# One layer of a hybrid decoder on one core: each SSD group's end in another order, and the q and k squares summed in two fp32r parts

## Chip, core and metric

One core of a Trainium2 chip runs the whole layer. The metric is the device time of one execution in microseconds (us). The kernel before took 1418.91 us, median of 3 runs (1418.65 to 1421.53).

## What is computed

512 prompt tokens and 8 sequences of 8 sample tokens (T = 576 columns in all) go through one layer. Cut to what matters here:

```python
h = rmsnorm(x, norm1_w); q, k, v, z, xbc, dt, ga, gb = split(h @ w_in)
q = rmsnorm(q per head of 64) * q_norm_w; k likewise       # first stage
attn = stick_breaking_attention(q, k, v)
xs, B, C = split(silu(causal_conv(xbc)))                   # width 4
y = ssd_chunked(xs, dt, A, B, C) + d_skip * xs             # 4 groups of 8 heads
y = rmsnorm(y * silu(z), per group of 512 channels) * ssd_norm_w
merged = sigmoid(ga) * (attn @ w_pa) + sigmoid(gb) * (y @ w_pb)
x = x + merged @ w_out; x = x + swiglu(rmsnorm(x)) @ w_down
```

## The kernel before

Channels lie on partitions and tokens along the free axis, in two halves of 288. A weight product is exact to nearly fp32: the weights are loaded as fp32, ScalarE copies them to fp32r (`w_hi`, L455, make_hi), VectorE subtracts to get the rest (`w_lo`, L461, make_lo), and TensorE adds hi*hi, hi*lo and lo*hi (L487, L488, L491). One tile of 128 output channels takes 8 slices of 6 matmuls of 288 columns. Output tiles alternate between two PSUM tiles (G), so tile t waits (`tile_free`) until tile t-2 was read. Small results rotate through four spare banks. Weight chunks have two buffers. make_hi(c+1) needs the products of chunk c-1 done, and TensorE begins a chunk when make_lo for it is done (`split`). Every engine runs its own list, strictly in the written order.

**First stage (L1173, L1805, L2400).** 13 tiles, of which 10 are q and k. For each of the 10, VectorE copies the tile to `pre` (L2407), ScalarE squares it (L1813), TensorE multiplies the squares with a matrix of ones of the head pair, in fp32 (L1152, norm_sums, two matmuls), and ScalarE makes the root (L1767, L1773). Per iteration ScalarE does: make_hi, root, square, split q. VectorE: make_lo, copy, norm, split q.

**Ahead of group 0.** The six conv inputs of group 0 (B, C, four x tiles; `group_inputs(0)`) are made as tiles. For each, GpSimd copies the saved 3-token heads (L955, conv_head) and, once ScalarE has put the tile into `conv_src` (L2031 to L2033), takes tails (L963, L965, conv_tail). VectorE convolves in 4 operations (L2570, L2572), ScalarE applies silu (L2003). GpSimd also stores the decay sums (L1015, L1016) and reads rows of them back (L995, L998, L1006), before the heads of the second conv input.

**A group (L1560).** by_token turns xs; the chunk steps c = 0 to 3 and the sample step mix small SSD products with slices of weight tiles that `ssd_plan` names. Its last two entries are the group's end. For groups 0 to 2, plan[4] is the conv inputs x2 and x3 of the next group. Plan[5] is two z tiles in group 0, and the double tile pb3 and one z tile in groups 1 and 2 (pb is y @ w_pb, 4+4 slices into two tiles). In the last group plan[4] is empty and plan[5] is pb2, pb3. The end runs so: TensorE: x2, outputs, x3, turn of the state (L1596), first tile of plan[5], the sums of y squared (L1607, 8 fp32 matmuls with `ones`), 4 slices of the next tile, by_token (L1431), in which the other 4 slices are mixed. VectorE: convolution of x2 and x3, gating y*z (L2770), make_lo and reads, y scaled (L2780), xdt (L2624), y_lo (L2787), make_lo, y begun (L2634), cb and decay products (L2638, L2671). ScalarE: squares (L2154), make_hi between the second and third, root (L2162, L2166), y_hi (L2171). At L1509 TensorE needs the decay product.

**Last group and what follows.** VectorE adds the stored gates (L2613, L2614; add_gated) for k = 2, 3 before y is scaled. GpSimd waits for all four of these (L1071), issues four loads (L1073) and the store of the state (L1075), then four stores of conv rows (L1080, L1081), waits until they have landed, loads x again (L1089, 2 MB, and L1090) and then the gates of k = 4, 5 (L1094), which VectorE needs at L2812. Only after that step comes make_lo of the first chunk of w_out and with it the output stage (L1632).

## Time and profile before

| | us |
|---|---|
| median of 3 runs | 1418.91 |
| the profiled execution, its own time | 1418.91 |
| its span | 1417.4 |
| TensorE busy | 1351.2 (95%) |
| VectorE busy | 963.0 (68%) |
| ScalarE busy | 707.4 (50%) |
| GpSimd busy | 263.5 (19%) |

The span is 1.5 us shorter than the execution's time. Busy times are unions of instruction spans. TensorE's matmuls overlap in the records (a record of 0.29 us follows the one before it by 0.13 us), so a stretch is read from start to start. A bracket at the end of a timeline row gives the idle time ahead of it and what ended it.

### The profile page before, as it was taken

Reading aid. Unit: us, or ns where it says so; the run is one execution under the profiler, and the core shown is the slowest. Engines: PE = TensorE matmul, PEld = TensorE weight load, DVE = VectorE, ACT = ScalarE, POOL = GpSimd, SP = SyncE. Lnnn points to the kernel's source line nnn. Section 1 sums busy time; section 2 is a strip of 40 time slices with the busy share of each in tenths; the row PEclk is TensorE's granted clock in tenths of the full one; section 3 lists DMA queues with packets and bytes.
Section 4 is the critical chain, followed back from the end, with each engine's and each line's share of the span. In section 5 each row is a group of like instructions: output and inputs, shape, how many; then the busy total and the mean of one; then the engine's idle time right before and its main releaser. Section 6 shows DMA issues by size and latency. Waiting matters only on the chain. (4 is left out here: it accounts for less than half of the span.)

```text
span 1417.4 us, 26926 instructions
## 1 busy us (share of the span) xinstructions
PE 1351.2 (95%) x10301; PEld 1257.5 (89%) x10301; DVE 963.0 (68%) x1569; ACT 707.4 (50%) x1271; POOL 263.5 (19%) x467
## 2 busy tenths in 40 slices
PE   5999999999999899999999999999999999999996
PEld 4998777899999898888888887899999999999996
DVE  4455546788853476787787776877899999983221
ACT  4576445777632354574464464535644444452221
POOL 4002233000021423333333324211100000000000
PEclk9999999999999999999999999999999999999998
DMA  4226665122255333334334425362333333323331
GB/s 122 75 77 193 180 209 163 56 71 71 71 159 166 75 86 109 95 96 116 107 95 124 109 68 176 111 204 75 90 90 90 104 105 90 90 71 98 97 95 36
DMA packets 200897, 152.86 MB, mean 108 GB/s; under 512 B 15529, under 2 KB 187585, under 8 KB 200720
## 3 DMA queue, kind: packets, MB, share of 16 engines
q1 hardware_dynamic: 175394, 97.93, 24.5%
q0 software_dynamic: 24992, 52.85, 12.7%
q8 instruction: 83, 1.36, 0.4%
q10 hardware_dynamic: 384, 0.37, 0.1%
q14 instruction: 44, 0.35, 0.1%
HBM read 127.80 MB, written 23.29 MB: 107 GB/s over the span
## 5 line engine op out<-in xcount | busy, mean ns | idle before, releaser
L487 PE MATMUL tile_banks<-x_hi,w_hi 128*128 128x288 f32 (+1 forms) x1232 | 368.1, 314 | 11.5 <-DVE w_lo L461 10.1
L488 PE MATMUL tile_banks<-x_lo,w_hi 128*128 128x288 f32 (+1 forms) x1104 | 309.7, 296 | 0.0
L491 PE MATMUL tile_banks<-x_hi,w_lo 128*128 128x288 f32 (+1 forms) x1232 | 262.4, 294 | 0.0
L487 PEld LDWEIGHTS tile_banks<-x_hi,w_hi 128*128 128x128 f32 (+1 forms) x1232 | 231.7, 188 | 25.2 <-DVE w_lo L461 12.4
L461 DVE TENSOR_TENSOR w_lo<-w_raw,w_hi 128x1024 fp32r<-128x1024 f32 (+2 forms) x125 | 150.5, 1204 | 113.0 <-ACT w_hi L455 112.4
L488 PEld LDWEIGHTS tile_banks<-x_lo,w_hi 128*128 128x128 f32 (+1 forms) x1104 | 207.7, 188 | 5.5 <-issue 3.6
L491 PEld LDWEIGHTS tile_banks<-x_hi,w_lo 128*128 128x128 f32 (+1 forms) x1232 | 197.5, 187 | 0.4
L455 ACT ACTIVATE w_hi<-w_raw 128x1024 fp32r<-128x1024 f32 (+2 forms) x125 | 129.5, 1036 | 99.2 <-PE tile_banks L491 94.0
L488 PE MATMUL tile_banks<-f_lo,w_hi 128*128 128x288 f32 x352 | 98.6, 294 | 0.0
L1102 POOL DMA_DIRECT2D out_y_prompt<-y_tok x8 | 6.2, 778 | 386.1 <-ACT y_tok L2315 373.3
L2203 ACT ACTIVATE w_hi<-sum_raw 128x512 fp32r<-128x512 f32 x71 | 44.9, 634 | 60.3 <-PE tile_banks L1674 24.6
L488 PEld LDWEIGHTS tile_banks<-f_lo,w_hi 128*128 128x128 f32 x352 | 66.1, 188 | 0.0
L2572 DVE SCALAR_TENSOR_TENSOR conv_acc<-conv_src,conv_par,conv_acc 128x600 f32<-128x600 f32 x72 | 62.1, 862 | 2.5
L886 POOL DMA_DIRECT2D v_page<-in_cache_v x64 | 34.4, 537 | 154.4 <-issue 154.4
L487 PE MATMUL tile_banks<-y_hi,w_hi 128*128 128x288 f32 x192 | 56.1, 308 | 0.3 <-DVE w_lo L461 0.3
L487 PE MATMUL tile_banks<-t_blocks,w_hi 128*128 128x288 f32 x192 | 54.7, 300 | 1.6 <-DVE f_lo L2931 1.5
L488 PE MATMUL tile_banks<-y_lo,w_hi 128*128 128x288 f32 x192 | 53.8, 295 | 0.0
L2836 DVE TENSOR_TENSOR w_lo<-sum_raw,w_hi 128x512 fp32r<-128x512 f32 x71 | 49.9, 703 | 5.5 <-ACT w_hi L2203 5.5
L2031 ACT ACTIVATE conv_src<-tile_banks 128x288 f32<-128x288 f32 x24 | 9.9, 411 | 87.2 <-PE tile_banks L491 87.2
L2437 DVE TENSOR_TENSOR_SCAN after_w<-rest,zero_col 128x128 f32<-128x128 f32 (+2 forms) x64 | 52.3, 817 | 0.3
L1064 POOL DMA_DIRECT2D out_ssm_sample<-old x32 | 25.5, 797 | 118.1 <-DVE old L2717 108.0
L2439 DVE TENSOR_TENSOR beta<-beta,after_w 128x512 f32<-128x512 f32 (+2 forms) x80 | 42.6, 532 | 2.8
(490 smaller groups left out, 3678.1 us busy)
## 6 DMA issues: line engine op xcount, KB each, us to landing
w_raw<-in_w_in SPq DMA_DIRECT2D x68, 512.0 KB, 4.0
k_page<-in_cache_k SPq DMA_DIRECT2D x64, 128.0 KB, 2.6
v_page<-in_cache_v POOLq DMA_DIRECT2D x64, 128.0 KB, 3.0
old<-in_state_ssm POOLq DMA_DIRECT2D x32, 256.0 KB, 3.5
out_ssm_sample<-old POOLq DMA_DIRECT2D x32, 256.0 KB, 2.9
w_raw<-in_w_pb SPq DMA_DIRECT2D x16, 512.0 KB, 3.5
w_raw<-in_w_down SPq DMA_DIRECT2D x16, 512.0 KB, 4.0
gates_dram<-gate_out POOLq DMA_DIRECT2D x22, 288.0 KB, 2.8
```

The source lines that it names most:

```text
L455: nc.scalar.activation(w_hi[:, c % 2, 0:tiles, 0:width], w_raw[:, c % 2, 0:tiles, 0:width], ACT.Copy).then_inc(hi_made, 1)
L461: nc.vector.tensor_tensor(w_lo[:, c % 2, 0:tiles, 0:width], w_raw[:, c % 2, 0:tiles, 0:width], f32(w_hi[:, c % 2, 0:tiles, 0:width]), ALU. ...
L487: nc.tensor.matmul(out, wh, xh[:, HALVES[h]], start=start and k == 0, stop=False, skip_group_check=onto)
L488: nc.tensor.matmul(out, wh, xl[:, HALVES[h]], start=False, stop=False, skip_group_check=onto)
L491: mm = nc.tensor.matmul(out, wl, xh[:, HALVES[h]], start=False, stop=stop and k == last, skip_group_check=onto)
L886: eng.dma_start(v_page[:, n % V_SLOTS, :], cache_v[0, bass.ds(page_of(eng, x, k), 1)].rearrange("o p h d -> p (o h d)")).then_inc(sem(f"v_ ...
L1064: eng.dma_start(states_of(ssm_sample, g, b), old[:, b % 2]).then_inc(sem(f"state_stored{b % 2}"), 16)
L2203: eng.activation(form_slot(f)[0], form_raw(f), ACT.Copy).then_inc(sem("form_hi_made"), 1)
L2437: link(eng.tensor_tensor_scan(out=after_w[:, slot, edge - width:edge][:, ::-1], data0=rest[:, slot, cols][:, ::-1], data1=zero_col[:, 0:1] ...
L2439: return eng.tensor_tensor(beta[:, x["u"] % 4, cols], beta[:, x["u"] % 4, cols], after_w[:, slot, edge - width + 1:edge + 1], ALU.mult)
L2572: ins = eng.scalar_tensor_tensor(out=dst, in0=src[:, w:w + m], scalar=conv_par[:, w * CT + ct:w * CT + ct + 1], in1=dst, op0=ALU.mult, op1 ...
L2836: eng.tensor_tensor(low, form_raw(f), f32(high), ALU.subtract).then_inc(sem("form_split"), 1)
```

## The change

Groups' ends: x3's convolution moves behind the gating and the squares; ScalarE writes the four squares into four places, VectorE adds them (3 additions), and TensorE sums once per half (2 fp32 matmuls, waiting for `y_summed`). They stand after 6 slices of the first tile of plan[5], and 5 slices of the next tile go ahead of by_token. make_lo of the next chunk moves ahead of y_lo, and y begun behind the first decay product. In the last group TensorE does 2 slices of pb3 ahead of the sums, and add_gated((2, 3)) moves to the end. First stage: the squares are made twice (fp32r and fp32), VectorE subtracts, and TensorE uses 4 fp32r matmuls. Ahead of group 0 GpSimd's list is interleaved. The cut diff (by_token's slices are in its second argument list; `y_squares` names four existing buffers; take_pb is the old read of a pb tile, one half at a time; begin_y is the old L2633 to L2635):

```diff
@@ -1010,19 +1015,27 @@
+early_keys = group_inputs(0)
+for key in early_keys[0:2]:
+    conv_head(key)
 eng.wait_ge(sem("sums_split"), 4)
...
-conv_io(group_inputs(0)[0])
+conv_tail(early_keys[0])
 eng.wait_ge(sem("sums_out"), 16 * 6)
-for st in range(2):
-    sums_in(st)
-eng.wait_ge(sem("picks_made"), 1)
+sums_in(0)
+conv_tail(early_keys[1])
+conv_head(early_keys[2])
+sums_in(1)
+conv_tail(early_keys[2])
+conv_head(early_keys[3])
+eng.wait_ge(sem("sums_hi_made"), 3)
 for g in range(2):
     picks_in(g)
-for key in group_inputs(0)[1:]:
-    conv_io(key)
+    conv_tail(early_keys[3 + g])
+    conv_head(early_keys[4 + g])
+conv_tail(early_keys[5])
@@ -1145,11 +1158,12 @@
 def norm_sums(n):
 
-    pe.wait_ge(sem("squared"), n + 1)
+    pe.wait_ge(sem("squares_split"), n + 1)
...
-        pe.matmul(spare(key)[:, 0:HALF], pair_ones[:, :], sq[:, n % 2, HALVES[h]]).then_inc(bank_full[use[key][0]], 1)
+        pe.matmul(spare(key)[:, 0:HALF], pair_ones_r[:, :], sq_hi[:, HALVES[h]], start=True, stop=False)
+        pe.matmul(spare(key)[:, 0:HALF], pair_ones_r[:, :], sq_lo[:, HALVES[h]], start=False, stop=True).then_inc(bank_full[use[key][0]], 1)
@@ -1556,9 +1570,9 @@
 around = before_groups[-1]
-gemm(around, range(0, 4))
+gemm(around, range(0, 6))
 for g in range(NG):
-    by_token(g, around)
+    by_token(g, around, {3: range(5, 6), 4: range(6, 8)} if g else {3: range(6, 7), 4: range(7, 8)})
@@ -1595,25 +1609,24 @@
+    last = g == NG - 1
     for key in before:
-        gemm(key, range(3, KD) if g == NG - 1 else range(KD))
-
-    for j in range(PG):
...
-            mm = pe.matmul(spare(key)[:, 0:HALF], ones[:, :], conv_acc[:, j % 2, HALVES[h]], start=j == 0, stop=j == PG - 1, skip_group_check=True)
...
-    last = g == NG - 1
-    for key in later if last else later[:-1]:
-        gemm(key)
-    around = None if last else later[-1]
-    gemm(around, range(0, 4))
+        gemm(key, range(3, KD) if last else range(0, 6))
+    if last:
+        gemm(later[0], range(0, 2))
+
+    pe.wait_ge(sem("y_summed"), (PG - 1) * (g + 1))
+    for h in range(2):
+        key = ("y_ss", g, h)
+        wait_read(pe, key)
+        pe.matmul(spare(key)[:, 0:HALF], ones[:, :], y_squares[0][:, HALVES[h]]).then_inc(bank_full[use[key][0]], 1)
+    if last:
+        gemm(later[0], range(2, KD))
+        around = None
+    else:
+        gemm(before[0], range(6, KD))
+        around = later[0]
+        gemm(around, range(0, 5))
@@ -1802,15 +1815,17 @@
+eng.activation(pair_ones_r[:, :], pair_ones[:, :], ACT.Copy).then_inc(sem("squared"), 1)
...
         wait_freed(eng, c)
-        if c >= 2:
-            wait_full(eng, ("ss", c - 2, 1))
-        eng.activation(sq[:, c % 2, :], pre[:, c % 2, :], ACT.Square).then_inc(sem("squared"), 1)
+        if c >= 1:
+            wait_full(eng, ("ss", c - 1, 1))
+        eng.activation(sq_hi[:, :], pre[:, c % 2, :], ACT.Square).then_inc(sem("squared"), 1)
+        eng.activation(sq[:, :], pre[:, c % 2, :], ACT.Square).then_inc(sem("squared"), 1)
@@ -2137,24 +2152,28 @@
-    before, later = plan[NC]
-    for key in before + later:
+    before, late = plan[NC]
+    for key in before:
         slot(key)
+    for key in late:
+        next_hi(key)
     before, later = plan[5]
     flush()
-    eng.wait_ge(sem("conv_done"), 6 * min(g + 2, NG))
-    key = ("state_out", g)
-    wait_full(eng, key)
-    eng.wait_ge(sem("y_added"), NC * (g + 1))
-    eng.activation(state_out[:, :, :].rearrange("p j n -> p (j n)"), spare(key)[:, :], ACT.Copy).then_inc(bank_read[use[key][0]], 1)
+    eng.wait_ge(sem("conv_done"), 6 * (g + 2) - 1 if g < NG - 1 else 6 * NG)
     for j in range(PG):
+        if j == 2:
+            key = ("state_out", g)
+            wait_full(eng, key)
+            eng.wait_ge(sem("y_added"), NC * (g + 1))
+            eng.activation(state_out[:, :, :].rearrange("p j n -> p (j n)"), spare(key)[:, :], ACT.Copy).then_inc(bank_read[use[key][0]], 1)
         eng.wait_ge(sem("y_gated"), PG * g + j + 1)
-        if j >= 2:
-            eng.wait_ge(sem("y_summed"), 2 * g + j - 1)
-        eng.activation(conv_acc[:, j % 2, 0:T], y_t[:, j, :], ACT.Square).then_inc(sem("y_squared"), 1)
-        if j == 1:
-            for key in before:
-                slot(key)
+        if j == PG - 1:
+            eng.wait_ge(sem("y_summed"), (PG - 1) * g + 1)
+        eng.activation(y_squares[j], y_t[:, j, :], ACT.Square).then_inc(sem("y_squared"), 1)
+    for key in before:
+        next_hi(key)
+    for key in late:
+        empty(key)
@@ -2164,6 +2183,9 @@
     eng.activation(y_rinv, y_root, ACT.Exp, scale=-0.5).then_inc(sem("y_rooted"), 1)
+    flush()
+    for key in before:
+        empty(key)
@@ -2412,6 +2434,9 @@
         split_lo(c - 2)
+    if c < KD + 2:
+        eng.wait_ge(sem("squared"), 2 * (c + 1) + 1)
+        eng.tensor_tensor(sq_lo[:, :], sq[:, :], f32(sq_hi[:, :]), ALU.subtract).then_inc(sem("squares_split"), 1)
@@ -2739,6 +2772,8 @@
+        if c == 0:
+            begin_y(g)
         outputs(g, c)
         if c == 0:
             xend_lo(g)
@@ -2753,12 +2788,12 @@
-    before, later = plan[NC]
+    before, late = plan[NC]
     for key in before:
         slot(key)
     outputs(g, NC)
-    for key in later:
-        slot(key)
+    for key in late:
+        make_lo(chunk_of[key] + 1)
@@ -2768,11 +2803,21 @@
         eng.tensor_tensor(y_t[:, j, :], y_t[:, j, :], z_s[:, j, :], ALU.mult).then_inc(sem("y_gated"), 1)
+    for j in range(1, PG):
+        eng.wait_ge(sem("y_squared"), PG * g + j + 1)
+        if j > 1:
+            eng.wait_ge(sem("y_summed"), (PG - 1) * g + j - 1)
+        eng.tensor_tensor(y_squares[0], y_squares[0], y_squares[j], ALU.add).then_inc(sem("y_summed"), 1)
     before, later = plan[5]
     for key in before:
-        slot(key)
-    if g == NG - 1:
-        add_gated((2, 3))
+        if key[0] == "pb":
+            take_pb(key, 0)
+        make_lo(chunk_of[key] + 1)
+    for key in late:
+        empty(key)
+    for key in before:
+        if key[0] == "pb":
+            take_pb(key, 1)
@@ -2781,13 +2826,20 @@
     if g + 1 < NG:
         scale_tokens(g + 1)
+        for key in later:
+            make_lo(chunk_of[key] + 1)
...
     ins.then_inc(sem("y_split"), 1)
+    if g == NG - 1:
+        for key in later:
+            make_lo(chunk_of[key] + 1)
     for key in later:
-        slot(key)
+        empty(key)
+    if g == NG - 1:
+        add_gated((2, 3))
```

## Rows read from the trace of the kernel before

**Rows 1.** The page: span.

```profile
span 1417.4 us, 26926 instructions
```

**Rows 2.** Waits of TensorE, whole span: total us, times, longest.

```profile
PE tile_banks L487 <- DVE w_lo L461: 11.4, 8, 4.2
...
PE spare_bank L1473 <- DVE old L2717: 4.9, 13, 0.4
```

**Rows 3.** L1152's count, and L1607 in group 0's end (timeline: start, us, what).

```profile
L1152 PE MATMUL spare_bank<-sq,conv_out x40: 403/404/408, 41.3 to 107.8; 128*128 128x288 f32 x40
...
608.31 2.10 PE L1607 MATMUL spare_bank<-conv_acc,ones 128*128 128x288 f32 x8
...
612.42 0.51 PE L487 MATMUL tile_banks<-x_hi,w_hi 128*128 128x288 f32 x1
```

**Rows 4.** Timeline of one period of the first stage.

```profile
55.93 1.14 PE L1152 MATMUL spare_bank<-sq,conv_out 128*128 128x288 f32 x4
...
58.27 0.67 ACT L1813 ACTIVATE sq<-pre 128x576 f32<-128x576 f32 x1
...
60.70 1.06 ACT L455 ACTIVATE w_hi<-w_raw 128x1024 fp32r<-128x1024 f32 x1
...
61.80 1.22 DVE L461 TENSOR_TENSOR w_lo<-w_raw,w_hi 128x1024 fp32r<-128x1024 f32 x1 [0.91 <-ACT w_hi L455]
...
63.23 1.14 PE L1152 MATMUL spare_bank<-sq,conv_out 128*128 128x288 f32 x4
```

**Rows 5.** Timeline ahead of group 0; its last row is a window's granted clock.

```profile
473.24 0.59 DVE L2570 TENSOR_SCALAR conv_acc<-conv_src,conv_par 128x600 f32<-128x600 f32 x1 [3.80 <-POOL conv_src L955]
...
477.65 0.61 PE L487 MATMUL tile_banks<-x_hi,w_hi 128*128 128x288 f32 x1 [4.21 <-DVE w_lo L461]
...
483.06 0.59 DVE L2570 TENSOR_SCALAR conv_acc<-conv_src,conv_par 128x600 f32<-128x600 f32 x1 [5.47 <-POOL conv_src L955]
...
487.49 0.40 PE L487 MATMUL tile_banks<-x_hi,w_hi 128*128 128x288 f32 x1 [1.94 <-DVE w_lo L461]
...
512.06 1.09 PE L1436 MATMUL spare_bank<-ident,xs_t 128*128 128x128 f32 x8 [1.73 <-ACT xs_t L2004]
...
478.00:480.00 2.00, 2.00 (x10) 0.50 0.60 143
```

**Rows 6.** Timeline of group 1's end and group 2's beginning.

```profile
711.04 0.60 PE L1596 MATMUL spare_bank<-ident,state 128*128 128x128 f32 x4
...
711.24 0.41 ACT L2031 ACTIVATE conv_src<-tile_banks 128x288 f32<-128x288 f32 x1 [3.30 <-PE tile_banks L491]
...
712.05 0.60 DVE L2570 TENSOR_SCALAR conv_acc<-conv_src,conv_par 128x600 f32<-128x600 f32 x1 [1.51 <-ACT conv_src L2033]
...
715.22 2.75 DVE L2770 TENSOR_TENSOR y_t<-y_t,z_s 128x576 f32<-128x576 f32 x4
...
717.79 1.05 ACT L455 ACTIVATE w_hi<-w_raw 128x1024 fp32r<-128x1024 f32 x1
...
734.21 0.40 PE L487 MATMUL tile_banks<-x_hi,w_hi 128*128 128x288 f32 x1 [1.12 <-DVE w_lo L461]
...
739.21 0.99 PE L1509 MATMUL spare_bank<-decay,xdt 128*64 128x128 f32 x14 [0.66 <-DVE decay L2671]
```

**Rows 7.** Timeline of the last group's end up to the output stage.

```profile
911.61 1.22 DVE L461 TENSOR_TENSOR w_lo<-w_raw,w_hi 128x1024 fp32r<-128x1024 f32 x1 [0.37 <-ACT w_hi L455]
...
911.84 4.18 PE L1607 MATMUL spare_bank<-conv_acc,ones 128*128 128x288 f32 x16
...
917.38 0.55 POOL L1073 DMA_DIRECT2D xs_t<-gated_dram  x1 [13.02 <-DVE pb_sum L2614]
...
933.89 0.76 POOL L1089 DMA_DIRECT2D x_again<-in_x_prompt  x1 [5.42 <-DMA out_conv_sample<-xend]
...
946.23 0.76 DVE L2812 TENSOR_TENSOR conv_acc<-conv_acc,conv_src 128x576 f32<-128x576 f32 x1 [0.86 <-DMA conv_src<-gates_dram]
...
952.98 0.37 PE L487 MATMUL tile_banks<-m_hi,w_hi 128*128 128x288 f32 x1 [1.44 <-DVE conv_acc L2804]
```

More of the change, by code:

```diff
@@ L256, in build @@
         pre = sb("pre", [P, 2, T], F32, qkv)
-        sq = sb("sq", [P, 2, T], F32, qkv)
+        sq = sb("sq", [P, T], F32, qkv)
+        sq_hi = sb("sq_hi", [P, T], F32R, qkv)
         root = sb("root", [P, T], F32, qkv)
@@ L265, in build @@
         k_out = sb("k_out", [P, 5, NKV * HD], F32, qkv)
+        sq_lo = sb("sq_lo", [P, T], F32R, qkv)
+        pair_ones_r = sb("pair_ones_r", [P, P], F32R, qkv)
         qkv.close()
@@ L332, in build @@
         y_rinv = decay[:, 0:5, :].rearrange("p h l -> p (h l)")[:, 0:T]
+        y_squares = [y_rinv, y_root, conv_acc[:, 0, 0:T], y_root]
         ssd.close()
@@ L1427, in gemm, with by_token @@
                         mm.then_inc(tile_done, 1)
-            def by_token(g, key_after):
+            def by_token(g, key_after, parts):
                 pe.wait_ge(sem("conv_done"), 6 * (g + 1))
@@ L1437, in by_token @@
                     mm.then_inc(bank_full[use[key][0]], 1)
-                    if c in (1, 3, 4):
-                        gemm(key_after, {1: range(4, 6), 3: range(6, 7), 4: range(7, 8)}[c])
+                    if c in parts:
+                        gemm(key_after, parts[c])
                 b_t, c_t = bc_t[:, g % 2, 0, :], bc_t[:, g % 2, 1, :]
@@ L2404, in _ @@
                     if c >= 2:
-                        eng.wait_ge(sem("squared"), c - 1)
+                        eng.wait_ge(sem("squared"), 2 * (c - 1) + 1)
                         eng.wait_ge(sem("normed_made"), c - 1)
@@ L2587, in empty, with take_pb @@
                 elif key[0] == "pb":
-                    _, g, n0 = key
                     for n in range(2):
-                        wait_tile(eng, t + n)
-                        dst = halves(pb_sum[:, n0 + n, :])
-                        if g == 0:
-                            ins = eng.tensor_copy(dst, tile(t + n))
-                        else:
-                            wait_freed(eng, tile_of[("pb", g - 1, n0)] + n)
-                            ins = eng.tensor_tensor(dst, dst, tile(t + n), ALU.add)
-                        ins.then_inc(tile_free[(t + n) % 2], 1)
+                        take_pb(key, n)
+            def take_pb(key, n):
+                t = tile_of[key] + n
+                _, g, n0 = key
+                wait_tile(eng, t)
+                dst = halves(pb_sum[:, n0 + n, :])
+                if g == 0:
+                    ins = eng.tensor_copy(dst, tile(t))
+                else:
+                    wait_freed(eng, tile_of[("pb", g - 1, n0)] + n)
+                    ins = eng.tensor_tensor(dst, dst, tile(t), ALU.add)
+                ins.then_inc(tile_free[t % 2], 1)
             def make_xend(g, c):
@@ L2632, in by_token @@
                     eng.wait_ge(sem("y_split"), g)
-                for j in range(PG):
-                    eng.tensor_scalar(y_t[:, j, :], xs_t[:, j, :], par[:, PAR_D + g * PG + j:PAR_D + g * PG + j + 1], None, ALU.mult)\
-                       .then_inc(sem("y_begun"), 1)
                 key = ("cb", g)
@@ L2652, in by_token, with begin_y @@
                                   ALU.mult).then_inc(sem("xend_f_made"), 1)
+            def begin_y(g):
+                for j in range(PG):
+                    eng.tensor_scalar(y_t[:, j, :], xs_t[:, j, :], par[:, PAR_D + g * PG + j:PAR_D + g * PG + j + 1], None, ALU.mult)\
+                       .then_inc(sem("y_begun"), 1)
             def xend_lo(g):
```

11 lines of the change are left out of this document (1 added, 10 removed).

## The prediction

> **What bounds the kernel now.** I read the page, TensorE's waits, then TensorE's timeline beside VectorE's, ScalarE's and GpSimd's at the places that the diff touches. TensorE is busy 1351.2 us (the table above) of a span of 1417.4 [rows 1], so work taken from it counts in full, unless a wait takes its place. Its waits are small and named: the largest sum, 11.4 us in 8 waits, is for the second part of the weights, the longest 4.2 us [rows 2]. Prices: a period of the first stage is 7.30 us [rows 4]. An fp32 matmul of 288 columns leaves two records. Group 0's sums, 16 records, end where the next product starts, 612.42-608.31 = 4.11 us, 0.51 per matmul [rows 3]. So two of them take 1.03, and a tile of 48 fp32r matmuls 7.30-1.03 = 6.27: 0.13 each, 0.78 per slice.
>
> **First stage.** Ten norm sums (40 records [rows 3] are 20 matmuls) go from 2 x 0.51 to 4 x 0.13: TensorE could save 0.51 each. But ScalarE gets a second square (0.6 to 0.67 [rows 4]) ahead of the weights' first part, and VectorE a subtraction of 576 columns, 0.69 (as one of the four of L2770 [rows 6]), ahead of the second. Now make_hi starts 4.77 after the sums begin and make_lo ends at 63.02, 7.09 after [rows 4]. The root comes 0.24 earlier (the first half's sum is ready after 0.26, not 0.51), so make_hi ends near +6.2, and make_lo at +7.45. TensorE would want that chunk at 6.27+0.52+0.52 = 7.3. Cover lost by 0.15 us, shared by two periods: the period is 6.9, saving 0.4 ten times, **-4.0** with one more small copy. Bounds: 0 if queues stretch the period to today's, -5.1 if nothing waits.
>
> **Ahead of group 0.** VectorE's first convolution starts at 473.24 after 3.8 us for GpSimd's head copy, the second at 483.06 after 5.5 us [rows 5]. Both heads now come before GpSimd's stores of sums. VectorE was free at 473.24-3.80 = 469.4; I give ScalarE's copies of the tile 0.4 more. A convolution takes 715.22-712.05 = 3.2 [rows 6] and make_lo 1.2 [rows 4], so TensorE, which arrives at 473.4 (477.65-4.21), starts at 474.4 and the next tile at 474.4+6.3 = 480.7 instead of 487.49 [rows 5]. That is 6.8: waits of 3.3 and 1.9, and 1.5 of clock. After the wait of 4.21 the granted clock is 0.50, the level of 1.2 GHz, and the tile from 477.65 to 485.55 takes 7.9, not 6.3 [rows 5]. The wait of 1.73 for the last silu [rows 5] is covered by two more slices, 1.57. GpSimd's reads of rows then come later, but are wanted only after by_token, 30 us on. **-8.3**; at the least -5, if heads 3 and 4 come late.
>
> **Groups 0 to 2, the sums.** Six fp32 matmuls less: -3.1 each. ScalarE's squares (0.65) and VectorE's additions (0.69) must be there when TensorE arrives. In group 1 VectorE was free at 712.05-1.51 = 710.5 [rows 6], where gating now starts: it ends 2.8 later at 713.3. Squares 1 and 2 are made meanwhile, then the copy of the state (0.6) and square 3 (713.9); the first addition ends at 714.0, square 4 at 714.7, the last addition near 715.5; TensorE arrives after 6 slices, 711.45+4.7 = 716.2. Hidden.
>
> **The same, what is late next.** x3's tile, which ScalarE now reads at 711.24 [rows 6], is read only after the four squares and make_hi (1.05 [rows 6]): squares end at 714.7, make_hi 715.7, three copies 716.5. The second half of pb3 uses the same PSUM tile and is wanted after 4 slices, 711.45+3.15 = 714.6: a **new wait of 1.9** in groups 1 and 2. Group 0 has a z tile there, in the other PSUM tile: none. The waits of 1.12 at 734.21 [rows 6], one like it in each of the three groups, go, since make_lo moves ahead of y_lo and is done 1.5 before TensorE's need. The silu of x3 ends at about 723.0, by_token wants it at 724.7: hidden by 1.7. The decay product: now TensorE is there at 739.21-0.66 = 738.55, 4.3 after 734.21 [rows 6]. In the new order y_lo, cb (0.7), b (0.8), xend (0.7) and the product (1.2) bring VectorE to 4.6 after the next group's first product (make_lo is done 1.5 before it, y_lo takes 2.75): a wait of 0.3, not 0.66. y begun (1.8) now stands between that product and VectorE's next work, which I expect 0.55 later; TensorE's short waits for VectorE there (13 of at most 0.4 [rows 2]) grow by 0.5 in groups 1 and 2. Group 0's end: -3.1-1.1-0.2 (an old wait within its sums, part of the 4.11) -0.5+0.5 = **-4.4**. Group 1: -3.1-1.1+1.9-0.3+0.5 = **-2.1**. Group 2: -3.1-1.1+1.9-0.3 = **-2.6**; there eight slices stand ahead of the decay product and hide y begun, and a wait of 0.3 goes. Bounds for each: -4.5 with no new wait, 0 if the new waits are double.
>
> **Last group.** make_hi for pb3's weights stood after the second square, so VectorE's second part started at 911.61, in time [rows 7]. Now it follows the fourth square, which follows the first addition: make_hi ends at 913.6, VectorE adds to 913.3, reads one half of pb2 (0.7), make_lo to 915.2. TensorE is ready at 911.84 [rows 7]: a new wait of 3.4, and the sums after 2 slices at 916.9. They take 1.0, to 917.9, and pb3 ends 6 slices on, at 922.6, 0.5 later than now. The root takes 1.4 and y scaled 3.0, to 922.3, y_lo to 925.0, make_lo 926.2, two reads 927.6, and only then the four operations of add_gated, 3.0: 930.6. GpSimd waits for that; now it goes on at 917.38 [rows 7]. Behind it stand in its list 4 loads (0.55 each), a store (0.8), 4 small stores (0.53 each), their landing (5.4 [rows 7]), and then x again: 930.8+10.5 = 941.4 instead of 933.89. The gates behind x again are awaited by VectorE until 946.23 already now [rows 7]. They come 7.5 later, and with them make_lo for the output stage: TensorE, ready at 952.98-1.44 = 951.5 now [rows 7] and 1.6 later then (pb3's tile is read only at 926.9), starts it near 960.4. **+7.4.** The idle of 7 us brings the low clock again: after 4.21 us it cost 1.5 [rows 5]; I take **+1.4**. After 3.4 idle us it may fall too; the later idle hides that except for 1.
>
> By the Trainium skill's page "TensorE: Matmul & The Clock Gate" (Part 1), half the clock is the idle state and sustained activity releases it. By that rule both pauses of the last group start cold; by rows 5 the first is open. The sum with both is 1407.
>
> **Sum.** -4.0-8.3-4.4-2.1-2.6+8.8 = -12.6, against the profiled execution's own 1418.91 (span 1417.4 [rows 1] and 1.5 around it), which is also the median of the runs: 1406.3, I say **1406**.
>
> **Rivals.**
> *A, the forecast* (0.52; its own range 1401 to 1411).
> *B, GpSimd's late list costs nothing.* Add_gated moved, but if x again and the gates were quick (their 12.3 us from issue to use [rows 7] are for 2.8 MB), the output stage starts after TensorE's own delay of 1.6. Then -12.6-8.8+1.6: 1399. For: TensorE waits there only 1.44 now. Against: VectorE waited for just this load. 0.17.
> *C, VectorE's and ScalarE's longer lists bind more.* The first stage keeps its period (+4.0), and each of three group ends keeps its 1.1 us wait (+3.3): 1413.6. For: both lists have under 1.5 us of room in a period. Against: that room is read off the same rows. 0.19.
> *D, hardly a difference*, C with the gain ahead of group 0 halved by GpSimd (+4.2): 1418. 0.07.
> *E, slower: the low clock stays.* Place: the output stage, after the long idle. Price: 0.5 us for every us at 1.2 GHz. Ahead of group 0 the tile after the wait lost only 1.5 us, what 3 us at half the clock cost [rows 5]. If it stayed low for its eight tiles, 8 x 6.3 = 50 us more: 1456. It turns the forecast over once the low level lasts about 25 us longer. Nothing in the rows shows such a length. 0.03.
> *F, the change doesn't act where it says*: the sums wait for VectorE so long that what six matmuls saved is idle. Each of four ends loses its 3.1, -12.6+12.4: about 1419, in "same". The additions end 0.7 before need, so 0.02.
>
> **Chances.** 0.2% is 2.8 us, about what a measurement of this kernel tells from no change: within 1416.1 to 1421.7 is "same". Faster: A, B, C 0.88; same: D, F 0.09; slower: E 0.03. The range takes A's bounds and most of B and C: 1398.5 to 1413; D to F and the rest of C and B, under 0.2, lie outside.
>
> **What would show it.** Right: L1152 with 40 records of 0.29 us, period 6.9; L1607's successor with 16 records in all; no wait of 4.2 and no clock of 0.50 ahead of group 0; TensorE waiting about 1.9 us for ScalarE's conv_src copies in groups 1 and 2, within pb3; 3.4 us for make_lo ahead of pb3 in the last group; L1073's successor waiting for pb_sum until 13 us later relative to the sums; and at the output stage's first product some 7 us of idle time and a granted clock of 0.5. Wrong: no wait at the output stage (B), a period near 7.3 (C), group ends without the 1.9 (faster by 4). The largest term is GpSimd's list in the last group; if one figure breaks the forecast it is that one.

## The result, and the profile after

The changed kernel takes **1410.82 us** (median of 4 runs, 1410.58 to 1412.5) beside 1418.85 for the kernel before in the same runs: ratio 0.9944, 95% interval 0.9930 to 0.9957, a gain of 8.0 us. I had forecast 1406, a gain of 12.6, with a range of 1398.5 to 1413. The profiled execution of the changed kernel is its slowest run, 1412.5 us, with a span of 1411.0, so the spans differ by 6.4 us only.

TensorE's waits of the changed kernel (engine, line, what it waited for: us in all, times, longest):

```profile
PE tile_banks L492 <- DVE conv_acc L2854: 7.1, 1, 7.1
...
PE tile_banks L492 <- DVE w_lo L466: 6.1, 5, 3.4
...
PE tile_banks L492 <- ACT conv_src L2048: 3.0, 2, 1.6
...
PE spare_bank L1523 <- DVE decay L2704: 2.2, 2, 1.1
...
PE tile_banks L492 <- DVE conv_acc L2856: 1.8, 1, 1.8
```

The sum for the weights' second part is 6.1 in 5 waits, 11.4 in 8 before [rows 2]. Ahead of group 0 the waits of 4.21 and 1.94 have become one of 0.77; of the three of 1.1 at the groups' ends two are gone, and the third, behind group 2, is 0.59. New are 7.1 us for L2854, which I had not forecast, 3.4 for pb3's weights and 3.0 for ScalarE's copies, which I had.

To place the difference I read the starts of the same instructions in TensorE's two timelines (us from the span's start; a stretch ends at the instruction that its row names, and the last two columns are us gained in it):

| stretch, up to | start before | start after | gained | forecast |
|---|---|---|---|---|
| first product of the first stage | 20.68 | 20.14 | 0.5 | 0 |
| first stage, to the turning of v | 114.38 | 110.88 | 3.0 | 4.0 |
| attention, to the decay sums | 465.59 | 460.94 | 1.1 | 0 |
| ahead of group 0 and by_token, to its first sample step | 530.12 | 516.32 | 9.2 | 8.3 |
| group 0's end, to group 1's first sample step | 632.03 | 613.87 | 4.4 | 4.4 |
| group 1's end | 741.13 | 721.31 | 1.7 | 2.1 |
| group 2's end | 853.60 | 832.31 | 1.5 | 2.6 |
| last group's steps | 903.78 | 883.10 | -0.6 | 0 |
| last group's end, to the output stage's second turning of x again | 959.38 | 952.96 | -14.3 | -8.8 |

Behind that point the rest of the span is as long as before, within 0.02 us. Up to the last group's end 20.7 are gained for 21.4 forecast; 1.6 of them lie in the two stretches that the change does not touch and are no merit of it, and 0.6 are lost again in the last group's steps, in a wait for a load of old states (1.59 us, 0.96 before) that has nothing to do with the change either. The stretches that it does touch gain 19.8. In the last group's end 14.3 are lost, not 8.8. That figure is an upper end: the profiled execution is the slowest of the four, and three kernels of the experiments that have the same last group (e8_ends, e12_begin_early, e4_empty_early) take 66.43, 67.42 and 68.15 us for this stretch, where the kernel before takes 55.60 and the changed one 69.86. So the loss is 10.8 to 14.3 us.

The first stage: periods of 6.86 to 7.10 us, mean (104.02 - 41.57)/9 = 6.94, 6.9 forecast, 7.31 before by the same reading. make_lo ends 61.42 + 1.23 - 55.29 = 7.36 us after the sums begin (7.45 forecast):

```profile
41.57 0.29 PE L1165 MATMUL spare_bank<-sq_hi,pair_ones_r 128*128 128x288 f32 x1
...
55.29 0.29 PE L1165 MATMUL spare_bank<-sq_hi,pair_ones_r 128*128 128x288 f32 x1
...
61.42 1.23 DVE L466 TENSOR_TENSOR w_lo<-w_raw,w_hi 128x1024 fp32r<-128x1024 f32 x1
...
104.02 0.30 PE L1165 MATMUL spare_bank<-sq_hi,pair_ones_r 128*128 128x288 f32 x1
```

Ahead of group 0 neither convolution waits for GpSimd now: the first starts when ScalarE has filled its tile, the second straight behind VectorE's work before it. TensorE waits 0.77 us where it waited 4.21 [rows 5]:

```profile
465.22 0.59 DVE L2595 TENSOR_SCALAR conv_acc<-conv_src,conv_par 128x600 f32<-128x600 f32 x1 [0.42 <-ACT conv_src L2048]
...
469.64 0.40 PE L492 MATMUL tile_banks<-x_hi,w_hi 128*128 128x288 f32 x1 [0.77 <-DVE w_lo L466]
...
469.72 0.59 DVE L2595 TENSOR_SCALAR conv_acc<-conv_src,conv_par 128x600 f32<-128x600 f32 x1
...
499.84 0.33 PE L1450 MATMUL spare_bank<-ident,xs_t 128*128 128x128 f32 x1 [0.29 <-ACT xs_t L2019]
```

Group 1's end (timeline): the squares, the additions, make_hi behind the fourth square, and only then the copies of x3's tile, for which TensorE waits 1.57 in pb3's second half; later the decay product, 1.09. The last row is behind group 2's end, where a wait for make_lo is left:

```profile
696.20 0.69 ACT L2172 ACTIVATE old_t<-y_t 128x576 f32<-128x576 f32 x1 [0.32 <-DVE decay L2810]
...
696.80 1.04 ACT L460 ACTIVATE w_hi<-w_raw 128x1024 fp32r<-128x1024 f32 x1
...
697.74 0.39 ACT L2046 ACTIVATE conv_src<-tile_banks 128x288 f32<-128x288 f32 x1
...
697.08 0.76 DVE L2810 TENSOR_TENSOR decay<-decay,old_t 128x576 f32<-128x576 f32 x1
...
698.55 0.40 PE L492 MATMUL tile_banks<-y_hi,w_hi 128*128 128x288 f32 x1 [1.57 <-ACT conv_src L2048]
...
719.38 0.88 PE L1523 MATMUL spare_bank<-decay,xdt 128*64 128x128 f32 x12 [1.09 <-DVE decay L2704]
...
830.60 0.40 PE L492 MATMUL tile_banks<-y_hi,w_hi 128*128 128x288 f32 x1 [0.59 <-DVE w_lo L466]
```

The last group's end, by engines: TensorE's waits of 3.43, 1.33, 7.05 and 1.76; VectorE's wait for the store of the state; GpSimd's list.

```profile
894.78 0.61 PE L492 MATMUL tile_banks<-y_hi,w_hi 128*128 128x288 f32 x1 [3.43 <-DVE w_lo L466]
...
897.83 1.28 PE L1622 MATMUL spare_bank<-decay,ones 128*128 128x288 f32 x4
...
908.08 0.37 PE L492 MATMUL tile_banks<-y_last_hi,w_hi 128*128 128x288 f32 x1 [1.33 <-DVE pb_sum L2626]
...
921.71 0.58 PE L492 MATMUL tile_banks<-y_last_hi,w_hi 128*128 128x288 f32 x1 [7.05 <-DVE conv_acc L2854]
...
945.01 0.37 PE L492 MATMUL tile_banks<-m_hi,w_hi 128*128 128x288 f32 x1 [1.76 <-DVE conv_acc L2856]
...
919.67 1.23 DVE L466 TENSOR_TENSOR w_lo<-w_raw,w_hi 128x1024 fp32r<-128x1024 f32 x1 [8.15 <-DMA out_ssm_prompt<-e_t]
...
938.25 0.76 DVE L2864 TENSOR_TENSOR conv_acc<-conv_acc,conv_src 128x576 f32<-128x576 f32 x1 [1.18 <-DMA conv_src<-gates_dram]
...
911.82 2.16 POOL L1086 DMA_DIRECT2D xs_t<-gated_dram  x4 [28.14 <-DVE pb_sum L2644]
...
913.98 0.77 POOL L1088 DMA_DIRECT2D out_ssm_prompt<-e_t  x1
...
921.29 0.76 POOL L1102 DMA_DIRECT2D x_again<-in_x_prompt  x1 [4.50 <-DMA out_conv_sample<-xend]
...
923.86 1.12 POOL L1107 DMA_DIRECT2D conv_src<-gates_dram  x2 [1.28 <-DVE conv_acc L2861]
```

GpSimd goes on at 911.82, after 28.14 us for L2644, the last operation of add_gated. It stores the state (L1088) at 913.98; VectorE, which awaits the landing of all four stores of a state ahead of the weights' second part for the last product's next chunk, waits 8.15 us for it, until 919.67; TensorE waits 7.05 us for what VectorE then reads. x again (L1102) is issued at 921.29. The granted clock in windows of 2 us behind the waits of 3.43, 7.05 and 1.76 (columns: window, us, busy and instructions of PE, PEld, DVE, ACT, POOL, then the clock, the DMA share, GB/s):

```profile
894.78:896.78 2.00, 2.00 (x8) 2.00 (x9) 0.61 (x1) 0.00 (x0) 0.00 (x0) 0.50 0.39 112
896.78:898.78 2.00, 2.00 (x11) 1.84 (x9) 0.00 (x0) 0.12 (x1) 0.00 (x0) 0.67 0.44 151
921.71:923.71 2.00, 2.00 (x8) 2.00 (x9) 1.92 (x4) 0.78 (x2) 0.87 (x2) 0.50 0.74 237
923.71:925.71 2.00, 2.00 (x11) 2.00 (x10) 1.81 (x3) 1.52 (x2) 1.12 (x2) 0.57 0.81 277
945.00:947.00 2.00, 1.99 (x11) 2.00 (x12) 1.97 (x4) 0.00 (x0) 0.00 (x0) 0.73 0.71 214
947.00:949.00 2.00, 2.00 (x11) 2.00 (x10) 1.97 (x3) 1.20 (x2) 0.00 (x0) 0.50 0.21 57
949.00:951.00 2.00, 2.00 (x16) 2.00 (x16) 1.73 (x3) 1.72 (x4) 0.00 (x0) 0.92 0.00 0
```

A window at 0.50, the level of 1.2 GHz, loses 1.0 of its 2 us. By that measure the three stretches lose 1.7, 1.9 and 1.7 us, 5.2 in all. That nearly closes the account of the last end: idle 13.57 us for 1.85 before (0.41 ahead of the last product, and 1.44 [rows 7]) is +11.7, the sums 0.90 for 3.80 are -2.9, the clock +5.2: 14.0 of 14.3. (The sums take 0.76 us in group 1, at full clock, so 0.1 of the clock's share is counted twice.)

### The profile page after: what moved, and what is told of

It is laid out like the page before. It is cut to its first block and busy times, and to the rows that moved or that the text cites. A ratio compares the mean times of both kernels' runs of the same rounds, so it can differ in the third digit from the quotient of the medians.

```text
span 1411.0 us, 26872 instructions
## 1 busy us (share of the span) xinstructions
PE 1339.1 (95%) x10253; PEld 1250.8 (89%) x10253; DVE 981.3 (70%) x1591; ACT 711.5 (50%) x1282; POOL 262.8 (19%) x467
## 3 DMA queue, kind: packets, MB, share of 16 engines
q0 software_dynamic: 24992, 52.85, 12.6%
## 5 line engine op out<-in xcount | busy, mean ns | idle before, releaser
L492 PEld LDWEIGHTS tile_banks<-y_hi,w_hi 128*128 128x128 f32 x192 | 36.7, 191 | 9.9 <-DVE w_lo L466 4.5
```

The costliest lines, as they stand in the source:

```text
L492: nc.tensor.matmul(out, wh, xh[:, HALVES[h]], start=start and k == 0, stop=False, skip_group_check=onto)
```

## The experiments

Theory 1: the last group's loss hangs on GpSimd's list, which add_gated at the end holds up, and on the clock that falls behind the waits. Theory 2: it comes of the new order of squares, additions and sums. "The same stretch" below is the last row of the table, from the last group's last step to the second turning of x again. Each kernel ran beside the kernel before, whose median was 1418.3 (the first four kernels, e1 to e4), 1418.6 (e5, e7, e8, e9), 1419.3 (e6, e10, e11) and 1418.9 (e12); the changed kernel's 1410.82 stood beside 1418.85. Differences between kernels that ran at different times are uncertain by a microsecond or two: the intervals of the ratios say how much.

**add_gated back ahead of y scaled (e1_gated_back).**

```diff
@@ last group, VectorE @@
+                if g == NG - 1:
+                    add_gated((2, 3))
                 eng.wait_ge(sem("y_rooted"), g + 1)
...
-                if g == NG - 1:
-                    add_gated((2, 3))
```

> The changed kernel with one thing undone: the last group's add_gated((2, 3)) stands ahead of y scaled again, in the 5.06 us in which VectorE waits for the root. Theory 1 (GpSimd's list, held up by add_gated at the end, costs the last group its gain): GpSimd's four loads start near 898.5 instead of 911.8, VectorE's wait of 8.15 us for the store of the state and TensorE's of 7.05 behind it go, x again is issued near 916 instead of 921.3, the output stage starts 9.4 us earlier, and with the low clock after the wait gone 1.5 more: 1410.8 - 11 = 1400, between 1398.5 and 1402. Theory 2 (the wait only hides one for the loads of x again and of the gates, which are as late either way because they wait for the conv rows): TensorE's 7.05 us turn up at the output stage instead, 1408 to 1411.

Measured: **1400.28** (1399.16 to 1401.49), ratio 0.9867 (0.9853 to 0.9882). GpSimd and TensorE:

```profile
899.18 2.16 POOL L1086 DMA_DIRECT2D xs_t<-gated_dram  x4 [14.97 <-DVE pb_sum L2644]
...
901.33 0.76 POOL L1088 DMA_DIRECT2D out_ssm_prompt<-e_t  x1
...
915.42 0.76 POOL L1102 DMA_DIRECT2D x_again<-in_x_prompt  x1 [4.11 <-DMA out_conv_sample<-xend]
...
908.74 0.37 PE L492 MATMUL tile_banks<-y_last_hi,w_hi 128*128 128x288 f32 x1 [1.33 <-DVE pb_sum L2626]
...
895.35 0.40 PE L492 MATMUL tile_banks<-y_hi,w_hi 128*128 128x288 f32 x1 [3.43 <-DVE w_lo L466]
```

No wait for L2854 is left, the output stage starts at 935.40, and the clock there is 1.00. It is theory 1, with its number: one operation group's place costs 10.5 us by the medians, and 11.7 in the traces (the same stretch takes 58.20 us, 69.86 in the changed kernel). The wait of 3.43 stands as in the changed kernel, with a fall of the clock behind it: these are the new order's doing, and with them the stretch is still 2.6 us longer than before. To that extent theory 2 is right too.

**The store of the state ahead of the wait (e2_store_first).**

```diff
@@ GpSimd, last group @@
+                wait_after_read(eng, ("state_out", g))
+                eng.dma_start(ssm_prompt[...], state_out[:, :, :]).then_inc(sem("stored_prompt_state"), 16)
                     eng.wait_ge(sem("gated_added"), 4)
                     for k in range(4, KD):
                         eng.dma_start(gated_a(k), gated_dram[k]).then_inc(sem("gates_in0"), 16)
-                wait_after_read(eng, ("state_out", g))
-                eng.dma_start(ssm_prompt[...], ...)
```

> The changed kernel with GpSimd's store of the last state put ahead of its wait for add_gated((2, 3)); add_gated stays at the end. It parts the two things that stand behind add_gated: the store of the state, which VectorE awaits ahead of the last product, and the loads of x again and of the gates of k = 4, 5. If only the store counts (theory 1a): TensorE's 7.05 us and 1.5 of low clock go, 1402. If the loads are as late as my prediction had it (theory 1b): the 7.05 us go, but x again is still issued near 920.5, the gates are there near 933 and the output stage starts near 940 instead of 945, after a wait of 5 to 6 us in front of it: 1405 to 1407. Theory 2 as in the run before: no gain, 1410 to 1411.

Measured: **1409.22** (1406.77 to 1410.38), ratio 0.9929 (0.9913 to 0.9945). The store goes at 892.21 and the 7.05 are gone, but TensorE waits at the output stage, as I had forecast for the change itself:

```profile
892.21 0.75 POOL L1084 DMA_DIRECT2D out_ssm_prompt<-e_t  x1 [7.01 <-ACT e_t L2168]
...
922.56 0.76 POOL L1102 DMA_DIRECT2D x_again<-in_x_prompt  x1 [5.25 <-DMA out_conv_sample<-xend]
...
935.42 0.76 DVE L2864 TENSOR_TENSOR conv_acc<-conv_acc,conv_src 128x576 f32<-128x576 f32 x1 [6.23 <-DMA conv_src<-gates_dram]
...
942.17 0.58 PE L492 MATMUL tile_banks<-m_hi,w_hi 128*128 128x288 f32 x1 [6.81 <-DVE conv_acc L2856]
```

The clock is 0.50 behind that wait too. It is mechanism 1b. By the medians the kernel gains 1.6 us where I expected 4 to 6, and its interval overlaps the changed kernel's; by the traces the same stretch takes 65.53 us, 4.3 less, as expected, and this execution had merely come into the last group 1.5 later (884.61 for 883.10). From x again's issue to the first use of the gates 12.86 us pass here and 12.34 before [rows 7], but 16.96 in the changed kernel. The two consequences of the late list lie one behind the other; taking one away shows the other.

**add_gated late in the kernel before (e10_late_add).**

```diff
@@ the kernel before, last group, VectorE @@
-                if g == NG - 1:
-                    add_gated((2, 3))
                 eng.wait_ge(sem("y_rooted"), g + 1)
...
                 for key in later:
                     slot(key)
+                if g == NG - 1:
+                    add_gated((2, 3))
```

> The kernel before with one thing of the change: add_gated((2, 3)) moved to the end of the last group. Theory: VectorE would end it near 928.8, GpSimd's four loads (2.2 us) and the store of the state follow, the store lands near 936.5, and VectorE, which waits for it ahead of the second part of the next weights (926.85 now), holds TensorE up by some 6 us at the last product's second tile; with 1.5 us of low clock behind the wait and x again and the gates later the output stage is 7 to 10 us later: 1418.6 + 8.5 = 1427, between 1424 and 1430. Rival: by its position alone it costs little, and the changed kernel's loss in the last group comes of the new order of squares, additions and sums: below 1421.

Measured: **1426.53** (1424.85 to 1428.24), ratio 1.0049 (1.0031 to 1.0067): 7.3 us slower. Its rows are those of the changed kernel:

```profile
930.88 0.76 POOL L1075 DMA_DIRECT2D out_ssm_prompt<-e_t  x1
...
936.36 1.23 DVE L461 TENSOR_TENSOR w_lo<-w_raw,w_hi 128x1024 fp32r<-128x1024 f32 x1 [8.13 <-DMA out_ssm_prompt<-e_t]
...
938.40 0.58 PE L487 MATMUL tile_banks<-y_last_hi,w_hi 128*128 128x288 f32 x1 [6.93 <-DVE conv_acc L2802]
```

So the place alone makes this wait, without the new order, and theory 2 is out for this part.

**Each part of the change alone (e7_ahead, e8_ends, e6_first_stage).** The kernel before with a part of the diff each (the hunks are those shown ahead of the prediction):

```diff
@@ e7_ahead: GpSimd ahead of group 0, TensorE @@
+early_keys = group_inputs(0) ... conv_tail(early_keys[5])
+gemm(around, range(0, 6))
+by_token(g, around, {1: range(4, 6), 3: range(6, 7), 4: range(7, 8)} if g else {3: range(6, 7), 4: range(7, 8)})
@@ e6_first_stage: sq_hi, sq_lo, pair_ones_r @@
+eng.activation(sq_hi[:, :], pre[:, c % 2, :], ACT.Square).then_inc(sem("squared"), 1)
+eng.tensor_tensor(sq_lo[:, :], sq[:, :], f32(sq_hi[:, :]), ALU.subtract).then_inc(sem("squares_split"), 1)
@@ e8_ends: all the rest @@
+gemm(around, range(0, 4))
+by_token(g, around, {3: range(5, 6), 4: range(6, 8)} if g else {1: range(4, 6), 3: range(6, 7), 4: range(7, 8)})
```

> The kernel before with GpSimd's interleaved list ahead of group 0 and six slices instead of four there, and nothing else. My theory by the traces (the deltas between the two kernels there, 7.6 us up to by_token and 1.6 in it): 1418.3 - 9.1 = 1409.2, between 1407.5 and 1411. As forecast -8.3: 1410. Rival: a part of the 9.1 comes from the loads of cached pages, which shift stage 2 by 1 to 2 us from run to run: 1411 to 1413.

> The kernel before with the groups' ends rebuilt and nothing else (q and k squares as before, GpSimd's list ahead of group 0 as before). By the traces groups 0 to 2 gain 4.0, 1.7 and 1.9 and the last one loses 14.3, of which the part behind the end is x again's: 1418.3 + 4 to + 7, so 1422 to 1425, slower than before. By my prediction's terms (-4.4 - 2.1 - 2.6 + 8.8 = -0.3): 1418. Rival: the end's rebuilding is a gain on its own and the first stage's change a loss: below 1416.

> The kernel before with the q and k squares in two fp32r parts, and nothing else. By the traces the mean period of the first stage falls from 7.31 to 6.94 us, 3.3 over nine periods, and 0.5 to 0.8 come back in the first iterations: 1418.6 - 2.7 = 1415.9, between 1415 and 1417; the same figure is what is left when the run with only the list ahead of group 0 (-9.1) and the one with only the groups' ends (+3.9) are taken from the whole change (-7.8). My prediction had -4.0: 1414.6. Rival: the longer lists of ScalarE and VectorE give all of it back, 1418.6.

| kernel | median, us | ratio, 95% interval | against before |
|---|---|---|---|
| ahead of group 0 | 1409.51 | 0.9939 (0.9921 to 0.9956) | -9.1 |
| groups' ends | 1422.49 | 1.0026 (1.0015 to 1.0036) | +3.9 |
| first stage | 1414.80 | 0.9966 (0.9954 to 0.9977) | -4.5 |

The groups' ends, the largest part of the diff, are a **loss** on their own: one late list costs more than six matmuls a group bring. The first two rows are as expected. The third is larger than the changed kernel's trace gave it, and nearer to my prediction; its interval goes from -3.3 to -6.5, and its own trace gains 3.9 in the stretch of the first stage (89.79 us for 93.70). The three add up to -9.7 against -8.0 for the whole, which those intervals allow. Where between 3.0 and 4.5 it lies stays open.

**Copies of x3's tile ahead of the fourth square (e4_empty_early).**

```diff
@@ ScalarE @@
                     if j == PG - 1:
+                        for key in late:
+                            empty(key)
                         eng.wait_ge(sem("y_summed"), (PG - 1) * g + 1)
...
-                for key in late:
-                    empty(key)
```

> The changed kernel with ScalarE's three copies of x3's tile ahead of the fourth square, not behind make_hi (groups 0 to 2). Theory: TensorE's waits of 1.57 and 1.41 us for these copies in groups 1 and 2 go whole, since the fourth square and the last addition then end about when TensorE reaches the sums: 1410.8 - 3.0 = 1407.8. Rival: the sums wait instead, since VectorE's last addition comes 1 us later: the waits move there and the time stays within 1 us of 1410.8.

Measured: **1406.99** (1403.92 to 1409.81), ratio 0.9915 (0.9900 to 0.9929). Both waits for L2048 are gone, and no wait stands at the sums (L1622), so the rival is out. Two waits grow in their place: the decay product's behind group 1's end from 1.09 to 1.58, and the one for make_lo behind group 2's end from 0.59 to 1.28:

```profile
721.28 1.09 PE L1523 MATMUL spare_bank<-decay,xdt 128*64 128x128 f32 x16 [1.58 <-DVE decay L2704]
```

By the starts the two ends gain 2.7 us more than in the changed kernel; the median says 3.8, with an interval that allows both.

**pb3's weights early in the last group (e3_hi_early), and with them pb2's first tile (e9_read_early).**

```diff
@@ ScalarE, last group: behind square j == 1 (moved up from behind the last square) @@
+                        next_hi(pb3)
@@ VectorE, last group (both moved up from behind the additions) @@
+                take_pb(pb2, 0)         (only e9_read_early)
                 addition j == 1
+                make_lo(pb3's chunk)
                 additions j == 2, 3
```

> The changed kernel, in the last group alone: make_hi of pb3's weights after the second square and make_lo after the first addition, as the old order had it. Theory: of TensorE's wait of 3.43 us ahead of pb3 some 1.3 are left, too short for the clock to fall to 0.50 (which cost 1.6 more over the next two slices and the sums); everything behind it, GpSimd's list too, comes 3.5 us earlier: 1407.3, between 1406.3 and 1408.5. Rival: the wait moves to the sums, which then wait for the last addition, and the gain is below 1 us: 1410.

> The changed kernel, in the last group alone: as in the run with make_hi and make_lo earlier (where TensorE still waited 3.33 us ahead of pb3, now for VectorE's read of pb2's first tile, at 893.31), and that read moved ahead of the first addition too. Theory: pb3's first product waits for two things, its weights and the PSUM tile that pb2's first half leaves; with both early the wait is about 1.0 us, the low clock behind it goes, and all that follows is 3.5 to 4 us earlier than in the changed kernel: 1407, between 1406 and 1408. Rival: the wait then moves to the sums, behind the last addition, and less than 1.5 us is gained: 1409.5.

Measured: **1408.68** (1408.49 to 1412.05), ratio 0.9937 (0.9920 to 0.9953), for the first, **1406.29** (1403.20 to 1408.84), ratio 0.9913 (0.9894 to 0.9932), for the second. TensorE at pb3's first product in the one and in the other:

```profile
893.31 0.37 PE L492 MATMUL tile_banks<-y_hi,w_hi 128*128 128x288 f32 x1 [3.33 <-DVE pb_sum L2630]
```

```profile
890.86 0.40 PE L492 MATMUL tile_banks<-y_hi,w_hi 128*128 128x288 f32 x1 [1.70 <-DVE w_lo L466]
```

In the first the weights were ready, and the wait stayed at 3.33 us, now for VectorE's read of the PSUM tile, which stood behind the additions: neither my theory nor my rival had it. Two things were late at one place, and the profile named only the later. That kernel's 2.1 us are not clear of the changed kernel's interval. With both early the wait is 1.70 (1.0 expected), the clock stays at 1.00 behind it, and 4.5 us are gained, as the theory had it (1406 to 1408).

**Three orders together (e5_three), and a fourth (e11_four).** e5_three is e1_gated_back, e4_empty_early and e9_read_early in one kernel; e11_four adds:

```diff
@@ VectorE, last group, behind y_lo @@
+                take_pb(pb3, 0)
                 make_lo(chunk of the last product)
-                take_pb(pb3, 0)
                 take_pb(pb3, 1)
```

> The changed kernel with three orders mended: add_gated((2, 3)) ahead of y scaled (alone 1400.3), x3's tile copied ahead of the fourth square (alone 1407.0), and pb3's weights and pb2's first tile early in the last group. Theory: they stand at different places and add up: 1410.8 - 10.5 - 2.8 - 3.8 = 1393.7, between 1392 and 1396. Rival: in the last group the conv rows' stores set when x again is loaded (issued at 915.42 in the run with add_gated back), so the gain ahead of pb3 comes back as a wait at the output stage: 1397 to 1398.

> The kernel with three orders mended (1396.2) and a fourth: in the last group VectorE reads pb3's first tile ahead of make_lo for the last product, not both tiles behind it. In that kernel TensorE waits 0.86 us ahead of the conv rows' transposes and 1.33 ahead of the last product, for this read, and the granted clock is 0.50 in the 2 us behind them. Theory: the second wait falls to 0.6 and the clock stays at 1.00: 1396.2 - 0.7 - 1.5 = 1394.0, between 1393 and 1395.5. Rival: the clock falls all the same, or the last product waits for its weights instead: 1395.5 to 1396.5.

Measured: **1396.19** (1393.48 to 1397.32), ratio 0.9835 (0.9815 to 0.9854), and **1395.55** (1394.33 to 1399.99), ratio 0.9840 (0.9818 to 0.9862). Both beat the kernel before and the changed one; e11_four beats e5_three by less than the measurement's uncertainty. e5_three lies just outside the 1392 to 1396 that I expected. Its rival is out: the wait at the output stage is 0.49 us. The three gains of 10.5, 3.8 and 4.5 would make 18.8; together they are 14.6. In e5_three TensorE waits 0.86 us for ScalarE ahead of the conv rows and 1.33 ahead of the last product, and the clock behind the two is 0.50 (e1_gated_back, with the same 1.33 alone, has 1.00). The wait of 0.86, which none of the three has alone, and the low clock (1.6 us by the measure above) are 2.5 of the 4.2 us that are missing; the rest I could not place, and it is within what the medians leave uncertain.

```profile
900.38 1.10 PE L1635 MATMUL spare_bank<-ident,conv_out 128*27 128x128 f32 x8 [0.86 <-ACT xdt L2203]
...
902.81 0.58 PE L492 MATMUL tile_banks<-y_last_hi,w_hi 128*128 128x288 f32 x1 [1.33 <-DVE pb_sum L2630]
```

The fourth order moved that second wait by 0.09 only, from the tile to the weights, and the clock fell all the same: it is the rival that came true.

**y begun ahead of the cb product again (e12_begin_early).**

```diff
@@ VectorE, by_token and the first chunk step @@
+                begin_y(g)
                 key = ("cb", g)
...
-                    if c == 0:
-                        begin_y(g)
                     outputs(g, c)
```

> The changed kernel with y begun (1.79 us on VectorE) ahead of the cb product again, as the old order had it. In the changed kernel TensorE waits 1.07 to 1.09 us in groups 1 and 2 for the decay product (I had forecast 0.3), and VectorE's xend product takes 1.49 us there where it took 0.67 before, beside GpSimd's b_seq (1.03 now, 2.79 before). Theory A (y begun's move is worth what it takes): the waits grow by 1.8 to 2.9 us in the three groups 1 to 3, less the 0.33 at the sample step: 1410.8 + 4.4 = 1415.2. Theory B (the slow xend product comes of the new order, and goes with it): its 0.82 comes back, the waits are 2.0: 1410.8 + 2 = 1412.8. Rival: VectorE has waited for its partners there anyway and the wait stays near 1.1: 1411.

Measured: **1410.60** (1408.98 to 1412.89), ratio 0.9940 (0.9926 to 0.9953). TensorE's waits at the beginning of group 1 are 0.95 and 0.76 (1.07 and 0.33 with y begun late), so by the traces the three ends lose 0.9, 0.3 and 0.4 us; in the profiled execution the output stage's wait is 0.48 and its clock did not fall, which hides it in the time. Neither theory A (1415.2) nor B (1412.8) came true in the time, which is the rival's (1411), though the waits did not stay as they were. By the traces moving y begun is worth about half a microsecond a group, below what a time can show.

## Why the prediction was right or wrong

**First stage, -4.0.** Right in mechanism (period 6.94 for 6.9, make_lo's end at 7.36 for 7.45); 3.0 in the trace, 4.5 (3.3 to 6.5) when made alone.

**Ahead of group 0, -8.3.** Right: 9.2 in the trace, 9.1 alone. TensorE waits 0.77 where I had 1.0, and the wait of 1.73 for the silu is 0.29.

**Groups 0 to 2, -4.4, -2.1, -2.6.** Measured -4.4, -1.7, -1.5. The new wait of 1.9 is there at 1.57 and 1.41, by the copies of x3's tile, as e4_empty_early shows by taking it away. Mis-sized is the decay product's wait behind groups 0 and 1, 0.3 forecast and 1.1 measured: the xend product takes 1.49 us, not the 0.67 that it took before, and that alone is the 0.8. Behind group 2's end, where no such wait stands, I let the wait for make_lo go whole, and 0.59 of it is left; the 0.5 that I gave y begun is there as a wait of 0.33 for xend_s in the first sample step of groups 1 and 2.

**Last group, +8.8.** This is the step that failed in size, by 5.5 us in the profiled execution (by 2.0 to 5.5 over the four traces with this last group), and in its place. *GpSimd's list* was right: x again was forecast for 941.4 in the old kernel's time, and 921.29 + 20.7 gained ahead of it is 942.0. But I let all that is late meet TensorE at the output stage. The list of things behind add_gated in my own sentence names the store of the state, and I did not ask who waits for its landing: VectorE does, ahead of the last product's next weights, so TensorE stood still 7.05 us there first and 1.76 at the output stage. The first wait also makes the second loads later: GpSimd issues the loads of the gates only when VectorE has merged the last product's first two tiles (L2861, a wait of 1.28 us), and from x again's issue to the gates' use pass 16.96 us (921.29 to 938.25), not the 12.34 that I carried over from the old kernel. Read along this path the miss is whole: x again 0.6 later than forecast, the loads 4.6, the clock 0.3. e2_store_first is the kernel in which my forecast's picture holds: 12.86 us for the loads, and 6.81 us of waiting at the output stage. *The clock* was taken at +1.4, once; in the profiled execution it fell three times, for 5.2 (twice in e8_ends, e12_begin_early and e4_empty_early, not at the output stage). I had written that after 3.4 idle us it may fall too, and let the later idle hide it; the later idle had another origin and hid nothing.

**Ahead of pb3, 3.4.** Measured 3.43. Its cause as I gave it, make_lo behind the additions, was half of it (e3_hi_early).

**Rivals.** B (the late list costs nothing) is out by e1_gated_back and e10_late_add. C (the longer lists bind more) is out for the first stage by its period and mostly out for the groups' ends, where of the three waits of 1.1 us only 0.59 is left. D, E and F are out: the gain ahead of group 0 is whole, the clock is back at full level within 6 us of each wait's end, and no wait stands at the sums. The measured time lay between the forecast and C for a reason that neither had. It is also nearer to the upper end of my range than to the forecast, and the range was wide; by its own words it was to take most of C, whose figure, 1413.6, lies above it.

## What to carry to other kernels

When an operation moves down one engine's list, write out everything that waits for it, then everything queued behind those waiters, and for each of these who awaits its landing; the first of them in time can hold up the others, and the one with the largest transfer need not be the first to be felt. A wait can have two causes of nearly the same length: take both away before its worth is judged. And a change that helps its own stretch (six matmuls a group) can lose more through one step that it moves out of an idle gap: of VectorE's 5.06 idle us ahead of the root, 3.0 had been filled by just that step.

## What the runs showed of the hardware

*Two operations that hinder each other.* GpSimd's b_seq and VectorE's xend product start within 0.1 us of one another in every group. In the kernel before, in groups 1 to 3, GpSimd's takes 2.8 us and VectorE's 0.67; in the changed kernel 1.03 and 1.49 (as in group 0 of every kernel); with y begun back (e12_begin_early) 2.80 and 0.67 again:

```profile
628.06 2.79 POOL L985 TENSOR_TENSOR b_seq<-b_hl,in_seq 96x512 fp32r<-96x512 f32 x1 [16.95 <-DVE b_hl L2644]
...
628.15 0.67 DVE L2650 TENSOR_TENSOR old_t<-xdt,end_decay 64x512 f32<-64x512 f32 x1
```

```profile
609.08 1.03 POOL L990 TENSOR_TENSOR b_seq<-b_hl,in_seq 96x512 fp32r<-96x512 f32 x1 [9.65 <-DVE b_hl L2671]
...
609.17 1.49 DVE L2677 TENSOR_TENSOR old_t<-xdt,end_decay 64x512 f32<-64x512 f32 x1
```

The Trainium skill's page "SBUF — State Buffer" (Who interferes with whom) has VectorE and GpSimd share a pair of ports under an exclusive lock, counts a VectorE instruction with two inputs in SBUF among those that contend with GpSimd's reads, and says that the order of issue decides who blocks. That one of the two is held up agrees with the rows. Which of them issued first the rows do not show: by its recorded start GpSimd's is first by 0.09 us in both kernels, and it is the slow one in the first. So the starts do not tell who will be held up; why the order of VectorE's earlier work decides it here stays open.

*The low clock by the length of the wait.* Behind waits of 3.3 us and more the granted clock fell in every trace from group 0 on, though not always at once (1.5 us after a wait of 3.43 in e2_store_first). Behind shorter ones it did not follow the length: 1.94 (the kernel before, ahead of group 0), 1.70 (e9_read_early), 1.51 (e7_ahead) and 1.27 (e4_empty_early) left it at 1.00; 1.76 (the changed kernel) and 1.80 (e6_first_stage, at the output stage) were followed by 0.50 about half a microsecond later, while another 1.80 in the same e6_first_stage, ahead of by_token, was not; 0.86 and 1.33 close together brought it down too (e5_three). The Trainium skill's page "TensorE: Matmul & The Clock Gate" (Part 1) says that the chip's watch on activity is free-running and that the point at which the clock changes varies with it; that the same wait can therefore meet it well or badly is my reading, with which these rows agree, and which they do not prove. Such a fall costs between 1.4 us (the kernel before, behind the wait of 4.21) and 2.9 (e8_ends, behind 3.43), by windows of 0.5 us, and times of kernels that differ by a microsecond or two may carry one or not.
